# A second plain column pair ahead of the seven-product blocks of a feed-forward layer, with the sums of x and one weight sum moved from GpSimd to VectorE

## The reference, cut to what matters

```
D_MODEL, SEQ, D_FF = 1024, 512, 2816
x = layer_norm(ALPHA * x + cross_attention(x, mem), ln2_g, ln2_b)
a, b = jnp.split(x @ w_ffn_in, 2, axis=-1)          # x 512 x 1024, w_ffn_in 1024 x 5632
h = (jax.nn.silu(a) * b) @ w_ffn_out                # 2816 x 1024
x = layer_norm(ALPHA * x + h, ln3_g, ln3_b)
```

## Time and profile before

| | us |
|---|---|
| median of 3 runs | 905.67 (905.16 to 905.96) |
| the profiled execution's own time | 903.1 |
| its span, first to last instruction | 901.1 |
| PE busy | 870.2 (97%) |
| DVE busy | 533.6 (59%) |
| ACT busy | 364.3 (40%) |
| POOL busy | 123.1 (14%) |

### The profile page before, as it was taken

The page is one execution under the profiler, slowest core; times in us unless marked ns, Lnnn a source line. Parts: engine busy times, 40 slices in busy tenths (PEclk is TensorE's granted clock), DMA queues, the critical chain, the costliest instruction groups (busy, mean ns, idle before and its releaser), DMA issues.

```text
span 901.1 us, 13484 instructions
## 1 busy us (share of the span) xinstructions
PE 870.2 (97%) x5239; PEld 757.5 (84%) x5239; DVE 533.6 (59%) x959; ACT 364.3 (40%) x738; POOL 123.1 (14%) x128
## 2 busy tenths in 40 slices
PE   8999999999999999999999995999999999999996
PEld 8988898877688888888889785999999999888885
DVE  4344357778524343526667699788788878422344
ACT  4112166148632222223345544455555555311221
POOL 3100000253200000000000143232222222000000
PEclk9999999999999999999999999899999999999999
DMA  8535532220013222336605110222222233433321
GB/s 280 159 94 140 118 95 73 93 94 2 1 48 94 93 94 93 97 105 251 200 1 188 47 48 1 94 94 95 94 95 94 95 104 108 162 98 104 108 89 70
DMA packets 70841, 90.38 MB, mean 100 GB/s; under 512 B 3181, under 2 KB 62391, under 8 KB 70783
## 3 DMA queue, kind: packets, MB, share of 16 engines
q1 hardware_dynamic: 70399, 89.15, 30.5%
q0 software_dynamic: 384, 0.43, 0.3%
HBM read 87.05 MB, written 2.52 MB: 99 GB/s over the span
## 4 chain that ended last, share of the span: by engine, by line
PE 87%; DVE 6%; issue 3%; ACT 2%; DMA 1%; SPq 0%; POOL 0%; DVEq 0%; POOLq 0%; ACTq 0%
PE ps L2087 19%; PE ps L2088 19%; PE ps L2089 19%; PE ps L2656 7%; PE ps L2658 7%; PE ps L2657 7%; PE ps L2252 3%; PE ps L2329 2%; PE ps L2289 2%; DVE w_lo L1964 2%; ACT w_hi L1311 1%; DMA x_nat<-in_x 1%; DVE resid L1795 1%; PE ps L2124 1%; PE ps L2704 1%
## 5 line engine op out<-in xcount | busy, mean ns | idle before, releaser
L2087 PE MATMUL ps<-xt_hi,w_hi 128*128 128x512 f32 (+1 forms) x368 | 143.1, 389 | 0.0
L2089 PE MATMUL ps<-xt_lo,w_hi 128*128 128x512 f32 (+1 forms) x368 | 142.4, 387 | 0.0
L2088 PE MATMUL ps<-xt_hi,w_lo 128*128 128x512 f32 (+1 forms) x368 | 142.3, 387 | 0.0
L1047 ACT CAST w_hi<-raw 128x1024 fp32r<-128x1024 f32 (+1 forms) x57 | 58.9, 1037 | 169.9 <-PE ps L2089 161.7
L1430 DVE TENSOR_TENSOR w_lo<-raw,w_hi 128x1024 fp32r<-128x1024 f32 (+1 forms) x57 | 68.9, 1210 | 90.7 <-ACT w_hi L1047 90.3
L2656 PE MATMUL ps<-xt_hi,w_hi 128*128 128x256 f32 x320 | 92.4, 289 | 12.7 <-DVE w_lo L1964 12.1
L2657 PE MATMUL ps<-xt_hi,w_lo 128*128 128x256 f32 x320 | 91.2, 285 | 0.0
L2658 PE MATMUL ps<-xt_lo,w_hi 128*128 128x256 f32 x320 | 91.1, 285 | 0.0
L1739 DVE TENSOR_TENSOR w_lo<-raw,w_hi 128x1024 fp32r<-128x1024 f32 x30 | 36.7, 1224 | 90.1 <-ACT w_hi L1214 90.1
L2087 PEld LDWEIGHTS ps<-xt_hi,w_hi 128*128 128x128 f32 x368 | 69.1, 188 | 14.5 <-issue 0.6
L2089 PEld LDWEIGHTS ps<-xt_lo,w_hi 128*128 128x128 f32 x368 | 69.1, 188 | 14.1
(11 more groups left out here) (345 smaller groups left out, 1971.5 us busy)
## 6 DMA issues: line engine op xcount, KB each, us to landing
raw<-in_w_in SPq DMA_DIRECT2D x24, 1024.0 KB, 5.0
raw<-in_w_ffn_in SPq DMA_DIRECT2D x40, 512.0 KB, 4.4
raw<-in_w_ffn_out SPq DMA_DIRECT2D x11, 1024.0 KB, 4.9
raw<-in_w_mix_out SPq DMA_DIRECT2D x4, 1024.0 KB, 4.9
raw<-in_w_branch_b SPq DMA_DIRECT2D x4, 512.0 KB, 3.9
resid<-in_x SPq DMA_DIRECT2D x1, 2048.0 KB, 9.4
raw<-in_w_xkv SPq DMA_DIRECT2D x2, 1024.0 KB, 5.5
raw<-in_w_ffn_in SPq DMA_DIRECT2D x2, 1024.0 KB, 5.8
```

The costliest lines, as they stand in the source:

```text
L1047: act.copy(hi, src).then_inc(hi_done, 1)
L2087: pe.matmul(dst, a_hi, b_hi, start=start, stop=False)
L2088: pe.matmul(dst, a_lo, b_hi, start=False, stop=False)
L2089: return pe.matmul(dst, a_hi, b_lo, start=False, stop=stop)
```

## The change

- `N_WHOLE = 2`: two pairs are computed in the plain way, and 18 blocks are left of 20. The second plain pair has 4 pieces of 24 matmuls on all 512 tokens; its operands go through `ffn_split` (ACT) and `ffn_rest` (DVE).
- x's sums are all on DVE. F22 is no longer stored: ACT copies the transposed right half of x from `ps` (`keep_x`), and DVE adds to it the other half straight from `ps` (`first_sum`, two calls make SUM1). POOL's `left_sums` is gone.
- T3 goes from POOL to DVE, right behind T2.
- In an even block ACT no longer runs `silu_left` before its copies for P4 and P5, nor `round_second` behind them; both stand in the odd block that follows. `hidden_rest(j, 1)` on DVE moves behind the rests of P2 and P7.
- The two halves of `op_slot` change places, and the waits count two pairs.

```diff
-N_BLOCK = 2 * (D_FF // P // 2 - 1)
+N_WHOLE = 2
+H_WHOLE = 2 * N_WHOLE
+N_BLOCK = 2 * (D_FF // P // 2 - N_WHOLE)
...
-            w = (w_hi, w_lo)[part][m % 4 // 2]
+            w = (w_hi, w_lo)[part][(m + 2) % 4 // 2]
...
             def weight_sums(n):                                     # POOL
...
                 pool.tensor_tensor(w_t1[:, :, :], w_quarter(n, 0, 1), w_quarter(n, 0, 0), ALU.subtract).then_inc(t1_done, 1)
-                pool.wait_ge(raw_in[n % 2], F_IN[n % 2] + 16 * (2 + n // 2))
-                pool.wait_ge(t1_done, n + 1)
-                pool.tensor_tensor(w_quarter(n, 0, 1), w_quarter(n, 1, 1), w_quarter(n, 0, 1), ALU.subtract).then_inc(t3_done, 1)
...
                 if n == 2 * TT:
-                    left_sums()
...
+            def ffn_split(i, q):                                    # ACT
+                p = PF + q
+                slot = q // 2
+                act.wait_ge(raw_in[slot], F_IN[slot] + 16 * (i + 1))
+                act.wait_ge(piece_done, 4 * i + p - 1)
...
+            def keep_x(t):
+                act.wait_ge(turn_lo, 4 * TT + 2 * t + 1)
+                act.copy(F21[:, :, at], ps[:, 2 * t, :].rearrange("p (k c) -> p k c", k=4)).then_inc(x_kept, 1)
...
                 op_round("P6", n)                                   # ACT, ffn_block
                 if odd:
+                    silu_left(n - 1)
                     silu_right(n - 1)
                 op_round("P2", n)
                 op_round("P7", n)
+                if odd and n > 1:
+                    round_second(j)
                 if not odd and n:
                     round_first(j)
                 hold_u2(n)
                 op_round("P1", n + 1)
                 if odd:
                     silu_second(n - 1)
-                else:
-                    silu_left(n)
                 op_round("P4", n)
                 op_round("P5", n + 1)
-                if not odd and n:
-                    round_second(j)
...
                 dve.tensor_tensor(w_t2[:, :, :], w_quarter(n, 1, 1), w_t1[:, :, :], ALU.subtract).then_inc(t2_done, 1)
+                dve.tensor_tensor(w_quarter(n, 0, 1), w_quarter(n, 1, 1), w_quarter(n, 0, 1), ALU.subtract).then_inc(t3_done, 1)
...
+            for q in range(4):                                      # PE, ahead of the blocks
+                if q == 0:
+                    pe.wait_ge(silu_done, 2)
+                if q == 2:
+                    pe.wait_ge(h_done, 2)
+                pe.wait_ge(lo_done, 4 + PF + q + 1)
+                for k in range(KT):
+                    ins = mm3(ps[:, q, :], wh[:, k, :], wl[:, k, :], xt_hi[:, k, :], xt_lo[:, k, :], k == 0, k == KT - 1)
+                ins.then_inc(piece_done, 1)
```

More of the change, by code:

```diff
@@ L646, in left_operand @@
             return x_sum({"P5": 1, "P6": 2, "P7": 3, "P3": 4}[kind], part)
-        F11, F12, F21, F22, SUM1, SUM2, SUM3, SUM4 = (sums[:, i, :, :] for i in range(8))
+        F11, F12, F21, SUM1, SUM2, SUM3, SUM4 = (sums[:, i, :, :] for i in range(7))
         def w_quarter(n, row, col):
@@ L868, in _ @@
                 sp.dma_start(gb[:, i, :], A[w][0:1, :].to_broadcast([P, D])).then_inc(gb_in, 16)
[L869 to L872, removed]
+            for i in range(N_WHOLE):
+                for q in range(2):
+                    sp.wait_ge(lo_done, i * 4 + (PF + 2 * q - 2))
+                    n0 = i * 256 + q * D_FF
+                    sp.dma_start(raw[q][:, :].rearrange("p (k c) -> p k c", k=KT),
+                                 w_f1[:, :, n0:n0 + 256]).then_inc(raw_in[q], 16)
             for n in range(N_BLOCK):
@@ L999, in widen_cross @@
                                  by_head.unsqueeze(3).to_broadcast([P, TT, 2, DH])).then_inc(recip_wide, 1)
[L1001 to L1008, removed]
             def weight_sums(n):
@@ L2040, in ffn_block @@
                     times_left(n // 2)
[L2042 to L2048 removed]
+            dve.wait_ge(turn_lo, 4 * TT + 4)
+            dve.tensor_tensor(F11, f32(xt_hi[:, 0:4, LO]), f32(xt_lo[:, 0:4, LO]), ALU.add).then_inc(x_whole, 1)
+            dve.tensor_tensor(F12, f32(xt_hi[:, 4:8, LO]), f32(xt_lo[:, 4:8, LO]), ALU.add).then_inc(x_whole, 1)
+            first_sum(2)
+            first_sum(3)
+            dve.wait_ge(sum_done, 2)
+            dve.wait_ge(x_whole, 2)
             dve.tensor_tensor(SUM2, SUM1, F11, ALU.subtract).then_inc(sum_done, 1)
[L2050 removed]
+            dve.tensor_tensor(SUM3, F11, F21, ALU.subtract).then_inc(sum_done, 1)
+            dve.wait_ge(sum_done, 4)
             dve.tensor_tensor(SUM4, F12, SUM2, ALU.subtract).then_inc(sum_done, 1)
+            first_hidden(0, 0)
+            ffn_rest(1, 0)
+            first_hidden(0, 1)
             sum_rest(1)
[L2053 removed]
+            ffn_rest(1, 1)
+            sum_rest(2)
+            ffn_rest(1, 2)
+            first_hidden(1, 0)
+            ffn_rest(1, 3)
+            sum_rest(3)
             op_rest("P1", 0)
             op_rest("P5", 0)
[L2056 removed]
             for n in range(N_BLOCK):
@@ L2059, in _ @@
                 if n == 0:
-                    first_hidden(1)
-                    sum_rest(3)
+                    first_hidden(1, 1)
                     sum_rest(4)
```

110 lines of the change are left out of this document (61 added, 49 removed).

## The result

| | before | after |
|---|---|---|
| median, us | 905.41 (904.21 to 905.96, 4 executions) | 884.04 (883.92 to 884.41, 4) |
| profiled execution, its span | 903.1, 901.1 | 883.92, 882.2 |
| PE, DVE, POOL busy, us | 870.2, 533.6, 123.1 | 867.8, 515.7, 82.7 |

The ratio is 0.9766 (95% interval 0.9749 to 0.9783): faster by 21.4 us.

The account below looks back on a forecast made before the run. PE, busy 97% of the span, was taken as the bound, so only its gaps and matmul count mattered. Gain 18.2 us takes the profiled execution from 903.1 to 884.9; plus 2.6 for the median gives 887.5, range 884.5 to 896.5.

Parts of the forecast that it names:

- The median of the runs is 2.6 above it; I keep that: Last term: 2.6 us from profiled execution to median, carried over from the kernel before, making 884.9 into 887.5.
- The sum for the profiled execution: P4 of block 16 at 743.5 instead of 761.73 us: gain 18.2, so 903.1 becomes 884.9 us.
- The norm step and PE's wait for the turn: Start: without POOL's left_sums the norm step takes 1.27 for 3.30 us; PE's wait goes, 1.3 us gained.
- The sums of x at nothing: Start: x's sums on DVE, about 7.3 us from 535.5 to 542.8, end before piece 2 and cost nothing.
- The gap before piece 0: Start of the second plain pair: its operand is ready at 546.1, PE free at 545.9; a 0.3 us gap.
- The second plain pair: Its four pieces of 24 matmuls add 21.8 us, with a 3.2 us gap before piece 3.
- the gap before piece 3: Second plain pair: its rest stands behind first_hidden(1, 0), so PE waits 3.2 us (1.2 to 4.5).
- the rival to which I gave 0.1: Clock falls again behind the gap before piece 3, costing 2.5 to 3.5 us: 890.5 us; chance 0.1.
- P6 of blocks 0 and 1: Chain seed, ACT copy and DVE rest still delay P6: 0.45 us each, 0.9 in all (0 to 2.4).
- The cover for T3: Blocks: T3's 0.68 us on DVE hides in DVE's wait for ACT's copy of T2; otherwise 12.3 us.
- The place of P4 of the last pair: P4 of block 16 starts at 743.5 us, where P4 of block 18 started at 761.73; gain 18.2 us.
- The rival on the other side, DVE as the bound: DVE sets the pace if T3 meets POOL's T1 every time: 24.7 us a pair, 926 us; chance 0.05.

Follow-up runs that it names:

- run 2: Changed kernel with the rest of piece 3 of the second plain pair moved ahead of first_hidden(1, 0) on DVE: 879.55 us, ratio 0.9735.
- run 3: Changed kernel with the weight sum T3 back on POOL, all else kept: 890.02 us, ratio 0.9854.
- run 4: Changed kernel with ACT's old order: silu_left and round_second back in the even block, hidden_rest(j, 1) ahead of the rests of P2 and P7: 889.36 us.
- run 5: Changed kernel with both T3 back on POOL and ACT's old order in the blocks: 894.50 us, ratio 0.9899.
- run 6: Changed kernel with only silu_left back in the even block, ahead of the copies for P4 and P5: 884.69 us, ratio 0.9787.
- run 7: Changed kernel with only round_second back behind the copies for P4 and P5 and hidden_rest(j, 1) ahead of the rest of P2: 882.65 us, ratio 0.9765.
- run 8: Changed kernel with x's two sums F11 and F12 back on POOL: 885.49 us, ratio 0.9793.
- run 9: Changed kernel run again without any edit: 884.23 us, ratio 0.9783.
- run 11: Changed kernel with one plain pair instead of two, block 0's P1 and P5 operands copied and split earlier, the rest kept: 879.29 us, ratio 0.9725.
- run 12: Changed kernel with piece 3's rest ahead of first_hidden(1, 0), second-pair operands copied as slots free, P6's copy ahead of block 0's seed: 878.42 us.
- run 1: Kernel before, unedited, profiled a second time: 904.31 us over 10 executions, ratio 1.0006; its profiled execution took 903.47 us.
- run 10: Kernel before with 62 extra unread matmuls filling PE's waits ahead of P1 and P7 of block 0: 901.04 us, ratio 0.9972.

## Why the prediction was right or wrong

**The step that failed** is in the sum: "The median of the runs is 2.6 above it; I keep that". The sum for the profiled execution was 884.9 and it took 883.92; the median of the changed kernel lies 0.1 above its profiled execution, not 2.6. The term was no constant that a kernel hands on to the next: in runs 2 to 9, 11 and 12 the median lies anywhere from 1.4 us below to 1.2 above the profiled execution, and 0.8 above it for the kernel before itself (run 1). Without this term the sum is 0.9 us off.

What makes the difference is shown in part. The kernel before spreads over 5.0 us (901.42 to 906.46 in 33 executions on three chips), the changed one over 0.5 in its first four and 2.5 in all eight (883.92 to 886.38). In the kernel before the longer executions tend to have the lower mean granted clock: of the 33 and the ten of run 1, the eight shortest (up to 902.13) show 0.992 to 0.995, the ten of 905.0 us and more 0.989 to 0.993, five of them 0.989. Filling the long waits of the start (run 10) took 2.9 us off the median and more than halved the spread to 2.1, so the start has a part in it. But the fall behind the gap of 5.28 us, with its 2.5 us, stands in both profiled executions, which were short ones; it can't be what the median has more than they. Run 1 shows what can: a further fall, behind a wait in a pair, that the first profile doesn't have. Where the long executions lose their time stays open, as no profile caught one. Not settled either: the first chip ran the kernel before at 905.4, the other three sets lie at 903.9 to 904.1, so 1.4 of the 21.4 us, and of the 2.6, go with that chip or day; the gain on the third chip is 19.8.

**Point by point.**
1. The norm step and PE's wait for the turn: right, and run 8 gives it back (1.3 us forecast; 885.49 against 884.2 in the medians, 1.55 by PE's starts).
2. The sums of x at nothing: right, with 0.54 us to spare.
3. The gap before piece 0: 0.33, forecast 0.3.
4. The second plain pair: the gap before piece 3 was 3.11, forecast 3.2, and its cause as said (run 2). The one wrong term here is the clock. Behind that gap PE's next nine starts lie 0.34 to 0.43 apart instead of 0.227, and it is 1.8 us until the steps are even again, of which 1.5 to 1.6 are the clock. This is the rival to which I gave 0.1, and its price, 2.5 to 3.5, was too high. The argument against it was that the first gap of 3.28 us had left the clock at 1.00; one case of a thing that goes both ways.
5. P6 of blocks 0 and 1: 0.44 and 0.29, forecast 0.9 for both.
6. The pairs: I kept 1.2 us of waits for them, and there are none. From 600 to 735 us the matmuls start 0.12 apart throughout, and a pair takes 20.16 us (forecast 20.2 to 20.5). The cover for T3 was there as read from the earlier trace rows.
7. The place of P4 of the last pair: the output product starts 18.9 us earlier, forecast 18.2. Of the 0.7 too little, 1.1 is the late start of the first profile, 1.2 the waits that are not there, 0.2 P6, less the 1.8 behind piece 3. (P1 of block 0 was put 20.5 us later; the prediction's own times give 20.4, and the sum doesn't use it.)

What I had not worked out is how the gain in the pairs divides. I read the wait off ACT's queue and gave T3's lock no number. Runs 3 to 5 show T3's move to be worth more than ACT's order (7.3 and 5.7 us in the blocks). The lock works through the same chain: it makes `h_lo` 0.3 us longer on average (run 3), and without it `silu_left` waits less for `h_lo` (run 4 against the earlier trace rows).

The rival on the other side, DVE as the bound, fell: DVE is busy 17.47 of 20.16 us in the pair shown and PE never waits. It was T1 beside T4 that stayed locked (1.78 us), T3 never was.

## What to carry to other kernels

- A difference between the profiled execution and the median is a term like any other, and not one to carry over: here it was 2.6 us, 0.8 in the second profile of the same kernel, and 0.1 in the changed one. Look at the mean granted clock of every execution beside its time. Where a kernel spreads, a profile tells one case of several.
- Where two engines share a lock, count the time of an operation in the queue of the other engine too, and follow it to who waits at the end of that queue. A call moved out of a tight stretch may show little or nothing alone and 5 us together with another one.
- Ahead of a wait for PE, queue everything that PE needs next. One pair of lines in another order (run 2) gave a fifth of the whole change once more.

## What the runs showed of the hardware

- **The clock behind a gap.** The same gap of 3.1 us before piece 3 stands in eight profiles. The granted clock fell to 0.50 behind it in five (the changed kernel twice, runs 6, 7 and 8) and stayed at 1.00 in three (runs 3, 4 and 5). From the start of piece 3 to P1 of block 0 it takes 7.06 to 7.22 us where the clock fell and 5.57 to 5.61 where it did not, so the fall costs 1.5 to 1.6. The Trainium skill, "TensorE: Matmul & The Clock Gate", section "Why this matters for your kernels", warns of idle gaps between bursts; the traces agree that it can happen, and show that it need not at this length. Nor is a gap of this length needed: in run 1 the clock fell behind a wait of 1.76 us, while it stayed at 1.00 behind waits of 1.83 (the first profile), 2.08 (run 10) and 2.16 us (run 5). What decides it wasn't found.
- **The lock of POOL and DVE**, measured both ways: the norm step 1.29 us alone and 3.30 beside POOL's sum (run 8), two rests 1.29 and 2.39 (run 3), a rest 0.68 and 1.60 (run 11). The Trainium skill, "SBUF — State Buffer", section "SBUF: two separate sides", states that a GpSimd operation and a VectorE one with two SBUF inputs lock each other out for a whole instruction, and these rows agree.
- **The same subtraction on either engine.** T3 of 128 by 512 elements takes 0.68 us on DVE and 1.47 on POOL, and on POOL it costs DVE up to 1.1 us of lock (2.39 less 1.29). So on the fuller engine it is nearly free: run 3 and the changed kernel differ in T3's place alone, and DVE is busy 514.9 us without the 18 instructions and 515.7 with them (514.5 in run 9).
